# One weight ring for the projection, the branch merge and the tail of a two-layer fp32 model

## What is computed

```
u = rmsnorm(x) @ w_in                      # 60 tiles of 128 columns: 28 "u", 32 "gates"
y_a, y_b, y_c, y_d = attention(u), pooling(u), state_space(u), recurrence(u)   # 512 wide each
merged = sum over 4 branches of sigmoid(gate_b) * (y_b @ w_branch_b)
x = x + merged @ w_out
x = x + relu(rmsnorm(x) @ w_ff1)**2 @ w_ff2
x = x + (p @ w_ple) * sigmoid(rmsnorm(x) @ w_ple_gate);  out = rmsnorm(x)
```

## Time and profile before

| | us |
|---|---|
| median of 3 runs | 3968.15 (3963.79 to 3968.45) |
| the profiled execution's own time | 3966.45 |
| its span | 3964.8 |
| mixers, about | 1680 to 2843 |
| merge, first to last matmul | 2858.94 to 3042.36 |
| tail, first to last product | 3056.55 to 3946.39 |
| TensorE (PE) busy over the span | 3649.5 (92%) |

### The profile page before, as it was taken

One profiled execution on the slowest core, in us unless ns is written; L12 is line 12 of the kernel. 1 busy time (PEld: TensorE's weight loads), 2 busy tenths in 40 slices (PEclk: granted clock), 3 DMA queues, 4 the chain that ended last, 5 costly groups with the idle time before them and its releaser, 6 DMA issues. The chain is left out here.

```text
span 3964.8 us, 43999 instructions
## 1 busy us (share of the span) xinstructions
PE 3649.5 (92%) x16724; PEld 2894.0 (73%) x16724; DVE 2188.0 (55%) x2464; ACT 1568.9 (40%) x2084; POOL 1096.9 (28%) x569
## 2 busy tenths in 40 slices
PE   7899988595999999789999999999798999999997
PEld 3678877464887878677777677777676888888886
DVE  5567547636888888756554222222245643353338
ACT  4321234534777777635122222222232332332234
POOL 1231220234111111134322122121243444444443
PEclk9899999796999999879999999999899999999999
DMA  5311256656999999843321311111354222323333
GB/s 195 95 48 67 74 168 217 214 168 234 378 398 402 401 397 403 346 176 136 143 77 59 109 63 60 60 62 57 117 186 143 93 94 97 100 91 96 98 114 124
DMA packets 176113, 650.33 MB, mean 164 GB/s; under 512 B 21392, under 2 KB 56560, under 8 KB 159824
## 3 DMA queue, kind: packets, MB, share of 16 engines
q1 hardware_dynamic: 134464, 553.24, 38.6%
q10 hardware_dynamic: 31696, 65.07, 4.4%
q0 software_dynamic: 9792, 29.81, 1.9%
HBM read 540.71 MB, written 107.34 MB: 163 GB/s over the span
## 5 line engine op out<-in xcount | busy, mean ns | idle before, releaser
L3730 POOL TENSOR_TENSOR t_wl<-t_raw,t_wh 128x1024 fp32r<-128x1024 f32 x160 | 386.1, 2414 | 522.8 <-ACT t_wh L3776 522.6
L100 PE MATMUL m_b<-b_high,m_high 128*128 128x512 f32 x960 | 405.1, 422 | 8.8 <-POOL m_low L2603 7.0
L102 PE MATMUL m_b<-b_high,m_low 128*128 128x512 f32 x960 | 383.0, 399 | 0.0
L101 PE MATMUL m_b<-b_rest,m_high 128*128 128x512 f32 x960 | 382.5, 398 | 0.0
L2601 POOL TENSOR_TENSOR m_high<-m_raw,m_one 128x1024 fp32r<-128x1024 f32 x60 | 120.8, 2014 | 788.7 <-PE m_b L102 725.2
L100 PE MATMUL t_b<-b_high,t_wh 128*128 128x512 f32 x768 | 301.9, 393 | 15.2 <-POOL t_wl L3730 15.2
L102 PE MATMUL t_b<-b_high,t_wl 128*128 128x512 f32 x768 | 299.6, 390 | 0.0
L101 PE MATMUL t_b<-b_rest,t_wh 128*128 128x512 f32 x768 | 299.5, 390 | 0.0
L3776 ACT ACTIVATE t_wh<-t_raw 128x1024 fp32r<-128x1024 f32 x160 | 169.2, 1057 | 312.5 <-PE t_b L102 291.9
L100 PE MATMUL zs_z<-zs_hs,zs_high 128*128 128x512 f32 (+1 forms) x584 | 226.8, 388 | 8.5 <-DVE zs_hs L310 8.0
L100 PEld LDWEIGHTS m_b<-b_high,m_high 128*128 128x128 f32 x960 | 185.5, 193 | 61.7 <-issue 11.7
(11 more groups left out here) (655 smaller groups left out, 8732.4 us busy)
## 6 DMA issues: line engine op xcount, KB each, us to landing
moe_raw<-in_expert_w SPq DMA_DIRECT2D x79, 2048.0 KB
ex_raw<-in_expert_w SPq DMA_DIRECT2D x39, 2048.0 KB
t_raw<-in_w_ff SPq DMA_DIRECT2D x128, 512.0 KB, 3.4
m_raw<-in_w_ug SPq DMA_DIRECT2D x60, 512.0 KB
yrows<-ex_y ACTq DMA_DIRECT2D x38, 512.0 KB
gates<-m_ob SPq DMA_DIRECT2D x32, 512.0 KB, 2.8
me_g<-gates SPq DMA_DIRECT2D x32, 512.0 KB, 3.7
zs_raw<-in_w_in_s SPq DMA_DIRECT2D x29, 512.0 KB
```

Source lines behind the costliest of these rows:

```text
L100: nc.tensor.matmul(out, w[0], x[0], start=first, stop=False)
L101: nc.tensor.matmul(out, w[0], x[1], start=False, stop=False)
L102: return nc.tensor.matmul(out, w[1], x[0], start=False, stop=last)
L3730: self.nc.gpsimd.tensor_tensor(self.wl[u % self.NW][:], self.raw[u % 2][:], self.wh[u % self.NW][:].bitcast(F32), ALU.subtract).then_inc(s ...
```

## The change

A class `Ring` takes the place of `Weights`. It is made once in `second_block`, ahead of the stages, with semaphores that live as long as the program, and numbers its tiles through mixers (0 to 59), merge (60 to 75) and the first two of the tail (76, 77). While a stage ends, SP loads and POOL splits the first two tiles of the next. A class `Ahead` holds a room of four tiles that stages of the mixers use one after the other for their scratch, and into which SP loads the first branch's `y` once the attention has read its inputs and the last gates have landed; ACT rounds it, half of it ahead of the attention's last copies, and DVE makes the remainder, all inside the mixers. The last merge unit is finished in two halves of 512 tokens. The tail takes its buffers from the ring and adds a third tile to each part. The attention's `cq` and `kr`, the state space's `z` and three of its `x`, and some scratch of others move into the room. Other operations, sizes and counts stay.

```
+class Ring:
+    def __init__(self, nc, s, life, size, parts):
+        self.nc, self.parts = nc, parts
+        self.raw = [s.sb(f"raw{j}", [P, size]) for j in range(2)]
+        self.high = [s.sb(f"high{j}", [P, size], F32R) for j in range(2)]
+        self.one, self.filled = s.sb("one", [P, 1]), life.sem("one_filled")
+        self.low = [s.sb(f"low{j}", [P, size], F32R) for j in range(2)]
...
+    def load(self, sp, n):
+        if n >= 2:
+            sp.wait_ge(self.split[n % 2], n // 2)
+        sp.dma_start(self.raw[n % 2][:], self.tile_of(n)).then_inc(self.w_in[n % 2], 16)
...
 # attention, ACT, last block of the last head
             if last:
+                if h == MH - 1:
+                    act.wait_ge(self.ahead.y_in, 16)
+                    F.W.done(act, N_UG - 1)
+                    self.ahead.round(act, range(2))
                 if h % 2:
                     pair(h // 2)
...
 # mixers, SP, GpSimd, ACT, DVE
                 for n in range(N_UG - 2, N_UG):
                     F.landed(sp, n)
+                lru.over(sp)
+                att.read(sp)
+                ahead.load(sp, 0)
                 att.over(sp)
...
-                for n in range(2, N_UG):
-                    F.halve(pool_, n)
+                for n in range(2, N_UG + 2):
+                    ring.halve(pool_, n)
...
                 F.take(act, N_UG * 2)
+                ahead.round(act, range(2, 4))
...
                 dve.wait_ge(F.taken, 2 * N_UG)
+                ahead.low(dve)
+                dve.wait_ge(ahead.y_low, 4)
...
 # merge, SP and GpSimd
-                sp.dma_start(yr[:], y_of(BRANCHES[0])).then_inc(y_in, 16)
                 for n in range(total):
-                    if n % 2 == 0:
...
+                    if n % 2 == 0 and n >= 4:
+                        W.load(sp, at + n // 2)
...
+                W.load(sp, at + total // 2)
+                W.load(sp, at + total // 2 + 1)
...
-                W.halve(pool)
+                for i in range(2, total // 2 + 2):
+                    W.halve(pool, at + i)
...
 # merge, DVE, the last unit
+                dve.wait_ge(gated, total)
+                dve.wait_ge(added, total - 1 - KD)
+                finish(total - 1, 0)
+                remainder(KD - 3)
+                finish(total - 1, 1)
+                remainder(KD - 2)
+                remainder(KD - 1, 0)
+                remainder(KD - 1, 1)
...
 # second_block
-        mixers(nc, A, R, C, (high, rest), gains)
-        merge(nc, A, R, high, rest)
-        tail(nc, A, R, C, out, high, rest, gains)
+        ring = Ring(nc, s, life, D, ((A["w_ug"], N_UG), (A["w_branch"], 2 * KD), (A["w_out2"], KD)))
+        with Stage(nc, "ah") as q:
+            ahead = Ahead(nc, q, life, R, (high, rest))
+            mixers(nc, A, R, C, (high, rest), gains, ring, ahead)
+            merge(nc, R, high, rest, ring, ahead)
+        tail(nc, A, R, C, out, high, rest, gains, ring)
...
 # tail
-        self.raw = [s.sb(f"raw{j}", [P, D]) for j in range(2)]
-        self.wh, self.wl = ([s.sb(f"{n}{j}", [P, D], F32R) for j in range(self.NW)] for n in ("wh", "wl"))
+        self.raw, self.wh, self.wl = ring.raw, ring.high + [s.sb("wh", [P, D], F32R)], ring.low + [s.sb("wl", [P, D], F32R)]
...
-            if i == 1:
+            if i == 2:
                 sp.dma_start(self.x[:, :, half(0)], tiles_of(self.R["xa"], 0)).then_inc(self.x_in[0], 16)
...
-        for u in range(self.NW):
-            high(u)
+        high(2)
```

More of the change, by code:

```diff
@@ L113, in __init__ @@
         self.low = [s.sb(f"low{j}", [P, size], F32R) for j in range(2)]
[L114 to L124, removed]
-        pool.wait_ge(self.filled, 1)
[L126 to L132, removed]
+        self.w_in, self.rounded, self.split, self.used = life.sems("w_in", 2), life.sem("rounded"), life.sems("split", 2), life.sems("used", 2)
@@ new lines, in tile_of, with fill, halve @@
+    def tile_of(self, n):
+        for w, count in self.parts:
+            if n < count:
+                return w[n]
+            n -= count
+    def load(self, sp, n):
+        if n >= 2:
+            sp.wait_ge(self.split[n % 2], n // 2)
+        sp.dma_start(self.raw[n % 2][:], self.tile_of(n)).then_inc(self.w_in[n % 2], 16)
+    def fill(self, pool):
+        self.nc.gpsimd.memset(self.one[:], 1.0).then_inc(self.filled, 1)
+    def halve(self, pool, n):
+        g, j = self.nc.gpsimd, n % 2
+        pool.wait_ge(self.filled, 1)
+        pool.wait_ge(self.w_in[j], 16 * (n // 2 + 1))
+        if n >= 2:
+            pool.wait_ge(self.used[j], n // 2)
+        g.tensor_tensor(self.high[j][:], self.raw[j][:], self.one[:].broadcast_to(self.raw[j].shape), ALU.mult).then_inc(self.rounded, 1)
+        pool.wait_ge(self.rounded, n + 1)
+        g.tensor_tensor(self.low[j][:], self.raw[j][:], self.high[j][:].bitcast(F32), ALU.subtract).then_inc(self.split[j], 1)
@@ L134, in tile, with ready, done @@
+    def ready(self, eng, n):
+        eng.wait_ge(self.split[n % 2], n // 2 + 1)
+    def done(self, eng, n):
+        eng.wait_ge(self.used[n % 2], n // 2 + 1)
     def tile(self, j, k):
@@ L2328, with __init__ @@
     NR = 3
-    def __init__(self, nc, s, q, A, R, C, high, rest, gains, banks):
+    def __init__(self, nc, s, q, A, R, C, high, rest, gains, banks, room):
         self.nc, self.A, self.R, self.C, self.h, self.gains = nc, A, R, C, (high, rest), gains
@@ L2584, in __init__ @@
         self.made = self.moved = self.parts = 0
[L2586 to L2603, removed]
     AHEAD = 3
@@ L2833, in __init__ @@
         self.inv, self.w, self.sc = q.sb("inv", [P, 4, PAD]), q.sb("w", [P, 4, P]), q.sb("sc", [P, 4])
-        self.d = [q.sb(f"d{j}", [P, SEQ]) for j in range(2)]
+        self.d = [room[:, j] for j in range(2)]
         self.got, self.u_in, self.pooled, self.summed, self.own, self.moved = (
@@ L3546, in _ @@
                     b, i = n // KD, n // 2
-                    pe.wait_ge(W.split[i % 2], i // 2 + 1)
+                    W.ready(pe, at + i)
                     if n >= 4:
@@ L3577, in _ @@
                         nc.scalar.activation(high[:, k], acc[:, k], ACT.Copy).then_inc(rounded, 1)
-                act.wait_ge(added, total - KD)
-                nc.scalar.activation(high[:, KD - 1], acc[:, KD - 1], ACT.Copy).then_inc(rounded, 1)
+                for c in range(2):
+                    cut = slice(c * BANK, (c + 1) * BANK)
+                    act.wait_ge(added, total - KD + c)
+                    nc.scalar.activation(high[:, KD - 1, cut], acc[:, KD - 1, cut], ACT.Copy).then_inc(rounded, 1)
             @block.vector
@@ L3588, in low, with remainder, finish @@
                         V.tensor_tensor(yl[b % 2][:, k], yr[:, k], yh[b % 2][:, k].bitcast(F32), ALU.subtract).then_inc(y_low, 1)
-                def remainder(k):
-                    dve.wait_ge(rounded, k + 1)
-                    V.tensor_tensor(rest[:, k], acc[:, k], high[:, k].bitcast(F32), ALU.subtract).then_inc(left, 1)
-                low(0)
-                for n in range(total):
+                def remainder(k, c=None):
+                    cut = slice(0, SEQ) if c is None else slice(c * BANK, (c + 1) * BANK)
+                    dve.wait_ge(rounded, k + 1 + (c or 0))
+                    V.tensor_tensor(rest[:, k, cut], acc[:, k, cut], high[:, k, cut].bitcast(F32), ALU.subtract).then_inc(left, 1)
+                def finish(n, c):
+                    cut = slice(c * BANK, (c + 1) * BANK)
+                    if c == 0:
+                        dve.wait_ge(first_half, 1)
+                    else:
+                        W.done(dve, at + n // 2)
+                    V.tensor_tensor(t[:, cut], g[n % 4][:, cut], ps[n % 4][:, cut], ALU.mult).then_inc(parted, 1)
+                    dve.wait_ge(parted, c + 1)
+                    V.tensor_tensor(acc[:, KD - 1, cut], acc[:, KD - 1, cut], t[:, cut], ALU.add).then_inc(added, 1)
+                for n in range(total - 1):
                     b, i, k = n // KD, n // 2, n % KD
@@ L3736, in tensor @@
                 continue
-            pe.wait_ge(self.split, i + 1)
+            if i < 2:
+                self.ring.ready(pe, self.FIRST + i)
+            else:
+                pe.wait_ge(self.split, i - 1)
             if i >= self.NB:
@@ L3891, in vector, with tail @@
         dve.wait_ge(self.final, 2 * KD)
-def tail(nc, A, R, C, out, high, rest, gains):
+def tail(nc, A, R, C, out, high, rest, gains, ring):
     with Stage(nc, "t") as s:
-        T = Tail(nc, s, A, R, C, out, high, rest, gains)
+        T = Tail(nc, s, A, R, C, out, high, rest, gains, ring)
         with nc.Block() as block:
```

136 lines of the change are left out of this document (75 added, 61 removed).

## The result

| | before | after |
|---|---|---|
| median of 17 runs each, us | 3967.55 (3963.79 to 3971.45) | 3975.56 (3970.4 to 3980.7) |
| ratio, 95% interval | | 1.0022 [1.0015, 1.0029] |
| the profiled execution, its span | 3966.45, 3964.8 | 3973.77, 3972.1 |

The kernel became 8.0 us slower, 0.2%, a hair over the 7.9 us up to which I had called it no change. Forecast were 3974.5 us: both pauses became shorter, and the tail's products took back more than that.

A forecast was written before the change was run, and what follows sets the result against it. Merge and tail were taken as TensorE-bound, time being matmul count times pace, with pauses between stages. Terms -4.6 - 4.35 + 15.4 = +6.45 us gave 3972.9 profiled, 3974.6 against the median, stated as 3974.5; range 3963 to 3981.

The forecast's parts named there:

- The tail's phases: Tail: operands 128 bytes out of phase slow matmuls by 6.67 ns each; +15.4 us, bounds 12 and 18.5.
- three slow kinds of units and one unchanged: Tail: b_high with tiles 0 and 1, b_high with third tile, DOWN with 0 and 1 slower; DOWN with third unchanged.
- four paces: Unit times before: first merge branch 5.545 us, last branch 5.60, tail 5.44, experts 5.58; source of the phase reading.
- Addresses cost nothing: Rival, chance 0.13: the pace belongs to something else of the stage, so the total is 3959.2 us, faster.
- First pause: Between mixers and merge: y loaded and rounded earlier, PE starts at about 2854.3 instead of 2858.94; -4.6 us.
- the rival on ACT's queue: Mixers' end, chance 0.27: load of y ahead of the attention's last copies takes over 9.3 us; total passes +7.9.
- +1.03: First pause: time from DVE's last remainder (2853.0) to the next stage, 1.03 us, giving 2854.1.
- One bound: First pause: if the load of y takes 11 us or more, the gain is gone.
- Second pause: Between merge and tail: halved last unit saves 1.4, POOL takes 4.0, PE starts 3052.2 instead of 3056.55; -4.35 us.
- the rival in which they do not meet: Merge's end, chance 0.10: POOL and DVE do not meet, second gap gives 7.6 us, total 3971.3.
- The clock: Behind both pauses, about 16 and 10 us long, PE's low clock (1.2 GHz) was to come as before.

The follow-up runs named there:

- before_low_out: Kernel before with one unused 4-byte tile between the tail's wh and wl, low tiles 128 bytes out of phase: 3981.53 us, 1.0037.
- before_high_out: Kernel before with only the tail's high weight tiles (wh) shifted by 128 bytes: 3987.78 us, 1.0055.
- phase_in: Changed kernel with the 4-byte column of ones allocated ahead of the gains, all weights and activations in one phase: 3950.36 us, 0.9958.
- more_sems: Changed kernel with 60 unused semaphores allocated in the merge, executed once: 3976.54 us.
- split_after: Changed kernel with tile 77 split on POOL at the tail's start instead of in the merge: 3970.92 us, 1.0007.
- early_y: Changed kernel with SP's load of the first branch's y issued ahead of the last gates' store: 3964.72 us, 0.9992.
- best: Changed kernel with ones column ahead of the gains, y load ahead of the last gates' store, tile 77 split in the tail: 3938.71 us, 0.9928.
- tail_shift: Changed kernel with an unused 128-byte tile ahead of the tail's own buffers, bringing them into phase with the ring's high tiles: 3970.22 us, 1.0008.

## Why the prediction was right

**The tail's phases: right in mechanism and size.** Forecast were three slow kinds of units and one unchanged, +18.5 us of products less 3.1 in stalls, +15.4. Measured were 5.55, 5.58, 5.61 and 5.44 us a unit, a tail longer by 15.25, and stalls shorter by 0.80, 0.66, 0.67 and 0.20 = 2.3, so 17.6 of products. Both terms were 0.8 to 0.9 high and cancel, so the 0.15 us between 15.4 and 15.25 is luck. before_low_out and before_high_out make the same cost in the untouched kernel by moving one kind of tile by 128 bytes, and phase_in removes it from the changed one. That the next weights count as well as the own ones, which I had read from four paces, is shown by before_high_out. "Addresses cost nothing" (0.13) is refuted. The cadence of the Trainium skill, "TensorE: Matmul & The Clock Gate", section "Wait — 56ns, not 53.3ns?", does not hold for these operands: no stretch of 512-column matmuls here ran at its 215.7 ns; the rows have 226.7 and 233.3.

**First pause: the mis-sized term.** I had -4.6 us, measured were -3.4. The load was right (7.76 for 7.8; the load of over 9.3 us of the rival on ACT's queue, 0.27, did not happen), and so was the chain to DVE's end (2852.57 for 2853.0, with PE's end 0.7 earlier). The step that failed is "+1.03" behind it: I took the exit of the merge's block for that of the mixers'. The mixers' exit takes 2.03 us in all eight traces with the ring, and in each of them the last store of `y` has landed before DVE ends (in the changed kernel at 2851.36 against 2852.57), so no store in flight makes it. more_sems shows that an exit grows by 7 ns with each semaphore. The mixers' exit clears 112 and the merge's 12, which makes 0.7 of the difference of 1.07 us by that price, an estimate; the rest stays open. One bound was worked out wrongly too: by the chain, the gain of 4.6 us is gone when the load takes 7.8 + 4.6 = 12.4 us, not 11.

**Second pause: a little more than forecast.** I had -4.35, measured were -5.1. DVE and POOL do take turns, and the rival in which they do not meet (0.10) is refuted: the remainders ended 8.06 us after the last matmul (forecast 8.5), and the exit took 0.96. split_after shows the price of the meeting: 3.1 us of pause.

**What I had not counted:** -0.7 us up to the mixers' last matmul, which is less than the traces differ there, and +1.5 us behind the tail's last product. Of these 1.5, 0.95 is the last sum on PE, two matmuls after the same 3.6 us of idling in both kernels, at the full clock before and at the low one after (below). The other 0.6 was not followed.

**The clock** was at its low level (1.2 GHz) behind both pauses, as forecast: 0.54 and 0.50 granted over the first 4 us, and still 0.63 behind the 7.76 us of early_y and 0.50 behind the 5.96 of split_after.

**Open in part:** in the mixers, phase_in should have given 12.6 us (120 units of 0.105) and gave 7.6; best gave 3.1. The stretches from the mixers' first matmul to their last, in after, phase_in and best, show where the rest went:

```profile
1679.40:2837.60 1158.20, 1092.34 (x4940) 835.45 (x4940) 471.39 (x852) 334.63 (x643) 295.07 (x142) 0.96 0.26 91
```

```profile
1684.10:2834.70 1150.60, 1081.51 (x4940) 831.08 (x4940) 473.19 (x852) 334.50 (x643) 296.37 (x142) 0.96 0.26 91
```

```profile
1681.60:2836.70 1155.10, 1086.93 (x4940) 834.63 (x4940) 473.04 (x855) 336.28 (x646) 296.02 (x142) 0.95 0.26 93
```

The same 4940 matmuls keep PE busy 10.8 us less in phase_in, and PE idles 3.2 us more (69.1 for 65.9): PE waits in many places of this stage, and part of the faster pace goes into longer waits. In best PE is busy only 5.4 us less, at a granted clock of 0.95 in place of 0.96. Why these waits grow, and why the clock was lower in best, was not tested.

## What to carry to other kernels

In a stretch that TensorE bounds, read the pace from start to start and compare it between stages: 3% of the pace, and 0.6% of this kernel's time, hung on a 4-byte tile allocated between two kinds of operands. So give all that a matmul reads one phase modulo 256 bytes, and recheck after every change of layout. When work is moved ahead into the end of a stage, look at what stands before it on its queue (here one store's wait held a load 23 us) and at which engines it will run beside: a split that is not yet needed is better placed where it meets nobody. An overlap can be a gain and still be hidden by the side effect of the same edit; undo each part alone before judging it.

## What was unexpected of the hardware

- A matmul of 512 fp32 columns starts 226.7 ns after the one before if operand and weights lie alike modulo 256 bytes, 233.3 ns if its own or the next weights differ by 128. It makes no difference which side is shifted: the weights (before_low_out) or the tail's own buffers with the hidden layer (tail_shift).
- The exit of a block, from DVE's last end to SP's first issue of the next block, took 0.96 us in one stage and 2.03 in another, and 60 more semaphores made it 0.41 longer.
- The same pause of 3.6 us ahead of the last two matmuls leaves the full clock in some kernels and the low one in others. The stretches of the two last sums, before and after:

```profile
3949.90:3951.20 1.30, 1.12 (x2) 0.30 (x2) 0.08 (x2) 0.61 (x1) 0.00 (x0) 1.00 0.00 0
```

```profile
3955.70:3957.90 2.20, 2.07 (x2) 0.50 (x2) 0.03 (x2) 0.58 (x1) 0.00 (x0) 0.50 0.00 0
```

It was low in five of the ten other kernels' traces as well and full in the other five. What decides it was not tested.
